# Attention logits in two pieces: key blocks 2 and 3 and then 0 and 1, in place of 1 to 3 and then 0

## The chip, the cores and the metric
The kernel runs on one core of one Trainium2 chip. The metric is the device time of one execution in microseconds; smaller is better. Engines are named as in the profile: PE is TensorE, ACT is ScalarE, DVE is VectorE, POOL is GpSimd, SP issues the DMAs.

## The reference
A decoder trunk of two layers over 512 tokens of width 1024, all in float32. Each layer is a half-step SwiGLU feed-forward, a mixer, and a second half-step feed-forward, each with its modulated RMS norm and gate. The mixer of layer 0 is a causal convolution module. The mixer of layer 1 is stick-breaking attention with 16 heads of width 64, and only this is touched:

```python
z = jnp.einsum('bhqd,bhkd->bhqk', qb, kf)
mask = (key_pos[None, :] < t[:, None])[None, None]
neg_log_keep = jnp.where(mask, jax.nn.softplus(z), 0.0)
rcs = lax.cumsum(neg_log_keep, axis=3, reverse=True)
suffix = jnp.concatenate([rcs[..., 1:], jnp.zeros_like(rcs[..., :1])], axis=-1)
a = jnp.where(mask, jnp.exp(jax.nn.log_sigmoid(z) - suffix), 0.0)
return jnp.einsum('bhqk,bhkd->bhqd', a, vf)
```

So each head needs the logits z, their softplus, a sum of the softplus over all later keys that the query may see, and one exponential.

## The kernel before, in words
Every matrix product is made of products of a high and a low part in the fp32r type. The kernel has one program for each engine, and an engine works through its own in order; semaphores join them. The order around the change is written out by hand.

**Layout.** Keys lie on the 128 partitions and queries along the columns. Key block c (c from 0 to 3) can be seen by the queries of its own block and of the later ones, so it has 512 - 128 c columns: 512, 384, 256 and 128, 1280 in all. One head's logits lie in three PSUM banks of 512 columns from z_base(t); odd and even heads t take different halves (banks 0 to 2 and 3 to 5), banks 6 and 7 take the output of the values. In SBUF a head's 1280 columns lie close together in sp_abs (two buffers, by t modulo 2), sp_hi, sp_lo (one each) and a_f (four, by t modulo 4).

**Pieces.** The columns of a head are worked on in two pieces, PIECE[0] and PIECE[1]. Before the change piece 0 is columns 512 to 1280 (blocks 1, 3 and 2, in banks 1 and 2) and piece 1 columns 0 to 512 (block 0, in bank 0).

**One head, piece by piece.**
1. TensorE, logits(t, p), L1823: mask matmuls write a very negative number on the diagonal blocks (L1843 two blocks at once, L1847 one), and two matmuls for each key block add the logits (L1853); z_done. It first waits until the exponential weights(t-2, p) has read the same banks (a_done).
2. The magnitude of z into sp_abs: of piece 0 by ScalarE's Abs (L904), of piece 1 by VectorE in magnitude(t) (L1450).
3. ScalarE: Exp (L908) and Ln (L910) on it, in place.
4. VectorE: softplus(t, p) (L1457) adds the positive part of z; sp_parts(t, p) splits the result into sp_hi (L1468) and sp_lo (L1470). Those of piece 0 wait until all of suffix(t-1) is done (cum_done).
5. TensorE, suffix(t, p), L1858: subtracts the softplus of the later keys from z, with sp_hi first and sp_lo second; L1864 takes the diagonal parts of two blocks in one matmul, L1867 all others; cum_done.
6. ScalarE, weights(t, p), L887: exp of what stands in PSUM then, into a_f; a_done.
7. TensorE, values(c2), L1873, once for two heads: the product with v (L1883). ScalarE (o_high, L881) and VectorE (o_low, L1474) split its result for the output projection.

**Order.** TensorE: for each t: logits(t+1, 0), suffix(t, 0), logits(t+1, 1), suffix(t, 1), and after an even t from 2 on values(t/2 - 1). ScalarE: for each t: Abs, Exp, Ln of piece 0, weights(t-1, 0), Exp, Ln of piece 1, weights(t-1, 1), and after an odd t from 3 on o_high. VectorE: for each t from 1 on: magnitude(t), softplus(t, 0), sp_parts(t, 0), softplus(t, 1), sp_parts(t, 1), then after an even t up to 10 split_qk (L1406, L1407) and after an odd t from 3 on o_low. For t = 0 magnitude and softplus(0, 1) stand ahead of sp_parts(0, 0). GpSimd computes the low part for split_qk (L647), and SP's DMAs (L541 to L552) bring q and k of the next two heads into stk, for which the next split_qk waits. The output projection (L1520 to L1522 with wsp[0]) follows suffix(15, 1) on TensorE, and SP loads its further weights after the last cum_done.

Of the kernel before, what the change touches and what calls it, by code (L numbers as in the profile page):

```python
# [25 lines left out]
P = 128  # L26
S = 512
# [27 lines left out]
GW = 512  # L55
NFFN = 4

PIECE = [slice(512, 1280), slice(0, 512)]
QL = S + (S - P) + P + (S - 2 * P)


# [38 lines left out]
def trunk(nc, x_in, up_in, down_in, mix_in, ada_in, mod_in, vec_in, dw_in, dwb_in, con_in, ind_in, sel_in, out):  # L100
    ctx = ExitStack()
    with ctx:
# [39 lines left out]
        with ExitStack() as scope:  # L142
            def ov(name, shape, dt=F32):
                return scope.enter_context(nc.sbuf_tensor(name, shape, dt))
# [24 lines left out]
        with ExitStack() as scope:  # L169
# [5 lines left out]
            a_f = ov("a_f", [P, 4, QL])  # L175
            qk = ov("qk", [P, 2 * KD, S])
            v_f = ov("v_f", [P, 4, D])
            con = ov("con", [P, 4, P], F32R)
# [38 lines left out]
        zps = ps[:, :, :].rearrange("p b s -> p (b s)")  # L217
# [121 lines left out]
        def z_base(t):  # L339

            return 3 * S * ((t + 1) % 2)

        def z_of(t, p):

            base = z_base(t)
            return zps[:, base + PIECE[p].start:base + PIECE[p].stop]

        def spread_bank(b):

# [308 lines left out]
        def _(act):  # L658
# [195 lines left out]
            def v_copy(s, c):  # L854
                if c < 3:
                    act.wait_ge(vchunk_done, 3 * (s // 11) + c + 1)
                else:
                    act.wait_ge(slab_done, N_QKV + s + 1)
                act.activation(v_f[:, c, S * (s // 11):S * (s // 11) + S], v_bank(s, c), ACT.Copy).then_inc(vf_done, 1)
# [23 lines left out]
            def weights(t, p):  # L883
                act.wait_ge(cum_done, 2 * t + p + 1)
                if t >= 4 and p == 0:
                    act.wait_ge(av_done, t // 2 - 1)
                act.activation(a_f[:, t % 4, PIECE[p]], z_of(t, p), ACT.Exp).then_inc(a_done, 1)  # L887

            act.add_instruction(mybir.InstLoadActFuncSet(
                name=nc.get_next_instruction_name(), engine=mybir.EngineType.Activation, act_func_set_id=EXP_LN_SET))  # L890
            for t in range(HEADS):
                if t == 0:
                    v_copy(11, 0)
                    v_copy(11, 1)
                    act.wait_ge(bc_done, 2 * KD)
                for p in range(2):
                    if t == 0 and p == 1:
                        v_copy(11, 2)
                    w = sp_abs[:, t % 2, PIECE[p]]
                    if p == 0:  # L900
                        act.wait_ge(z_done, 2 * t + 1)
                        if t >= 2:
                            act.wait_ge(splo_done, 2 * (t - 2) + 1)
                        act.activation(w, z_of(t, 0), ACT.Abs).then_inc(ln_step, 1)  # L904
                        act.wait_ge(ln_step, 5 * t + 1)
                    else:
                        act.wait_ge(abs_done, t + 1)
                    act.activation(w, w, ACT.Exp, scale=-1.0).then_inc(ln_step, 1)  # L908
                    act.wait_ge(ln_step, 5 * t + 2 * p + 2)
                    act.activation(w, w, ACT.Ln, bias=ones[:, 0:1]).then_inc(ln_step, 1)  # L910
                    if t == 0 and p == 1:
                        v_copy(11, 3)
                    if t >= 1:
                        weights(t - 1, p)
                if t % 2 and t >= 3:
                    o_high((t - 3) // 2)
# [12 lines left out]
        def _(dve):  # L929
# [517 lines left out]
            def magnitude(t):  # L1447

                dve.wait_ge(z_done, 2 * t + 2)
                dve.tensor_scalar(sp_abs[:, t % 2, PIECE[1]].bitcast(U32), z_of(t, 1).bitcast(U32), SIGNLESS, None,  # L1450
                                  ALU.bitwise_and).then_inc(abs_done, 1)

            def softplus(t, p):

                w = sp_abs[:, t % 2, PIECE[p]]
                dve.wait_ge(ln_step, 5 * t + 2 * p + 3)
# [3 lines left out]
            def sp_parts(t, p):  # L1460

                w = sp_abs[:, t % 2, PIECE[p]]
                if t == 0 and p == 0:
# [53 lines left out]
        def _(pe):  # L1517
# [296 lines left out]
                    pe.wait_ge(vf_done, 4)  # L1814
                pe.matmul(spread_bank(b), sel[:, b % KD, :], y_both[:, :], start=True, stop=True).then_inc(bc_done, 1)

            at_key = [0, S, 2 * S, 2 * S - P]

            def span(base, c, q0):

                return slice(base + at_key[c] + q0 - P * c, base + at_key[c] + S - P * c)

            def logits(t, p):  # L1823


                base = z_base(t)
                blocks = ((1, 3, 2), (0,))[p]
                c2, half = t // 2, t % 2
                at = stk[c2 % 2]
                pe.wait_ge(stk_s[c2 % 2], 96 * (c2 // 2 + 1))  # L1830
                if half == 1:
                    pe.wait_ge(stkq_s[c2 % 2], 32 * (c2 // 2 + 1))
                if t == 0:
                    pe.wait_ge(conr_done, 2)
                    pe.wait_ge(qkn_done, 2 * KD)
                    pe.wait_ge(vf_done, 4)
                if t == 1:
                    pe.wait_ge(vf_done, 7)
                if t >= 2:
                    pe.wait_ge(a_done, 2 * (t - 2) + p + 1)  # L1840
                if p == 0:
                    diagonals = zps[:, base + S:base + 2 * S].rearrange("p (n q) -> p n q", n=4)[:, 0:4:3, :]
                    pe.matmul(diagonals, con[:, 0, :],  # L1843
                              con[:, 1, :].rearrange("p (n q) -> p n q", n=1).broadcast_to((P, 2, P)),
                              start=True, stop=False, skip_group_check=True)
                first = base + at_key[(2, 0)[p]]
                pe.matmul(zps[:, first:first + P], con[:, 0, :], con[:, 1, :], start=True, stop=False,  # L1847
                          skip_group_check=True)
                for c in blocks:
                    keys = slice(P * c, P * (c + 1))  # L1850
                    seen = slice(P * c, S)
                    for part in range(2):
                        last = pe.matmul(zps[:, span(base, c, P * c)], at[:, half, keys],  # L1853
                                         at[:, 2 + 2 * half + part, seen], start=False, stop=False,
                                         skip_group_check=True)
                last.then_inc(z_done, 1)

            def suffix(t, p):  # L1858

                base = z_base(t)  # L1860
                for part in (sp_hi, sp_lo):
                    pe.wait_ge(sphi_done if part is sp_hi else splo_done, 2 * t + p + 1)
                    if p == 0:
                        pe.matmul(zps[:, base + S:base + 2 * S], con[:, 2, :], part[:, S:2 * S], start=False,  # L1864
                                  stop=(part is sp_lo), skip_group_check=True)
                    for c, later in (((1, 2), (1, 3), (2, 2), (2, 3)), ((0, 0), (0, 1), (0, 2), (0, 3)))[p]:
                        last = pe.matmul(zps[:, span(base, c, P * later)],  # L1867
                                         con[:, 2 if later == c else 3, :],
                                         part[:, span(0, later, P * later)],
                                         start=False, stop=(part is sp_lo), skip_group_check=True)  # L1870
                last.then_inc(cum_done, 1)

            def values(c2):  # L1873

                pe.wait_ge(a_done, 4 * c2 + 4)
                if c2 == 0:
                    pe.wait_ge(vf_done, 8)
                if c2 >= 2:
                    pe.wait_ge(o_done, c2 - 1)
                for c in range(4):  # L1880
                    for half in range(2):
                        cols = slice(P * c2 + HD * half, P * c2 + HD * (half + 1))
                        last = pe.matmul(ps[HD * half:HD * half + HD, 6 + c2 % 2, P * c:S], v_f[:, c, cols],  # L1883
                                         a_f[:, (2 * c2 + half) % 4, span(0, c, P * c)], start=(c == 0), stop=(c == 3),
                                         skip_group_check=True)
                last.then_inc(av_done, 1)

            for s in range(12):
                n = N_QKV + s
# [38 lines left out]
            for t in range(HEADS):  # L1928
                for p in range(2):
                    if t + 1 < HEADS:  # L1930
                        logits(t + 1, p)
                    suffix(t, p)
                if t % 2 == 0 and t >= 2:
                    values(t // 2 - 1)
# [77 lines left out]
```

## Time and profile before

| | us |
|---|---|
| median of 3 runs | 1951.51 |
| lowest, highest | 1951.27, 1951.62 |
| the profiled execution | 1952.25 |
| its span in the profile | 1950.4 |
| granted TensorE clock, mean | 0.999 |

The profile is one execution, and its span leaves out some 1.9 us around the instructions. In the timeline a row is a run of instructions of one line: its start, its time, the engine, the line, and how many; the mean of a group of matmuls is longer than the distance between two of them, since they are pipelined. The attention's head loop runs from about 1447 to 1540 us.

### The profile page before, as it was taken

The page shows a single profiled execution, that of the slowest core. Times are in us where ns is not written, and L with a number is a line of the kernel's source. Part 1 is how long each engine was busy: PE and PEld are TensorE (multiplying, and loading weights), DVE is VectorE, ACT ScalarE, POOL GpSimd, SP SyncE. Part 2 cuts the span into 40 slices and gives each one's busy share as a digit, 9 for nine tenths or more (in the row PEclk, how much of TensorE's full clock was granted, in tenths as well). Part 3 has the DMA queues.
Part 4 walks back from the last instruction along what each step waited for, and adds up shares of the span by engine and source line. Part 5 has one row for each costly group of instructions (what it writes and reads, how often), then busy time and mean ns, then how long its engine had stood idle before and what let it go on. Part 6 is the DMA issues. An engine that isn't in the chain of part 4 may idle for free.

```text
span 1950.4 us, 23638 instructions
## 1 busy us (share of the span) xinstructions
PE 1923.8 (99%) x9211; PEld 1553.7 (80%) x9211; DVE 1075.6 (55%) x1323; ACT 663.4 (34%) x744; POOL 150.9 (8%) x101
## 2 busy tenths in 40 slices
PE   6999999999999999999999999999999999999999
PEld 5888888876578888888888888887777788888887
DVE  4655555589877555533756553255579673333322
ACT  4423222242354222322422222224259653232211
POOL 0100001121411000001100000111022030000000
PEclk9999999999999999999999999999999999999999
DMA  9455554536313555533255552232245323222232
GB/s 393 161 190 197 194 181 143 188 114 179 107 66 119 202 186 199 169 115 99 98 194 185 202 178 90 101 124 97 86 119 130 104 81 108 100 94 99 76 103 87
DMA packets 59992, 275.86 MB, mean 141 GB/s; under 512 B 8480, under 2 KB 9120, under 8 KB 43168
## 3 DMA queue, kind: packets, MB, share of 16 engines
q1 hardware_dynamic: 56864, 270.88, 41.0%
q10 hardware_dynamic: 3072, 4.23, 0.9%
q8 instruction: 36, 0.59, 0.1%
q14 instruction: 20, 0.16, 0.0%
HBM read 251.94 MB, written 2.10 MB: 130 GB/s over the span
## 4 chain that ended last, share of the span: by engine, by line
PE 93%; DMA 2%; DVE 2%; ACT 1%; issue 1%; SPq 1%; ACTq 0%; POOL 0%; DVEq 0%
PE ps L1520 27%; PE ps L1521 27%; PE ps L1522 27%; PE ps L1761 2%; PE ps L1541 2%; DMA raw<-up_d 1%; PE ps L1548 1%; PE ps L1867 1%; PE ps L1883 1%; PE ps L1560 1%; PE ps L1561 1%; PE ps L1566 1%; PE ps L1853 1%; DMA stage<-ada_d 1%; SPq L492 0%
## 5 line engine op out<-in xcount | busy, mean ns | idle before, releaser
L1520 PE MATMUL ps<-h_hi,w 128*128 128x512 f32 x1552 | 606.0, 390 | 1.1 <-DVE h_lo L1033 1.1
L1521 PE MATMUL ps<-h_lo,w 128*128 128x512 f32 x1552 | 604.0, 389 | 0.0
L1522 PE MATMUL ps<-h_hi,w 128*128 128x512 f32 x1552 | 603.9, 389 | 0.0
L1520 PEld LDWEIGHTS ps<-h_hi,w 128*128 128x128 f32 x1552 | 291.3, 188 | 68.9 <-issue 7.9
L1522 PEld LDWEIGHTS ps<-h_hi,w 128*128 128x128 f32 x1552 | 291.3, 188 | 60.8
L1521 PEld LDWEIGHTS ps<-h_lo,w 128*128 128x128 f32 x1552 | 291.3, 188 | 59.9
L933 DVE TENSOR_TENSOR w<-raw,w 128x1408 fp32r<-128x1408 f32 (+1 forms) x104 | 201.0, 1932 | 207.9 <-ACT w L664 207.8
L664 ACT ACTIVATE w<-raw 128x1408 fp32r<-128x1408 f32 (+1 forms) x104 | 164.7, 1584 | 414.9 <-PE ps L1522 403.4
L1520 PE MATMUL ps<-g_hi,w 128*128 128x512 f32 x704 | 273.9, 389 | 0.0
L1521 PE MATMUL ps<-g_lo,w 128*128 128x512 f32 x704 | 273.9, 389 | 0.0
L1522 PE MATMUL ps<-g_hi,w 128*128 128x512 f32 x704 | 273.9, 389 | 0.0
L725 ACT ACTIVATE act_tmp<-ps 128x512 f32<-128x512 f32 x84 | 50.2, 597 | 547.6 <-PE ps L1522 531.5
L940 DVE SCALAR_TENSOR_TENSOR ada_raw<-ada_raw 128x1024 f32<-128x1024 f32 x128 | 163.3, 1276 | 96.1 <-DMA ada_raw<-mod_t_d 96.1
L1133 DVE TENSOR_TENSOR act_tmp<-act_tmp,ps 128x512 f32<-128x512 f32 x84 | 57.8, 688 | 280.2 <-ACT act_tmp L725 280.2
L1141 DVE TENSOR_TENSOR w<-raw,w 128x2048 fp32r<-128x2048 f32 x76 | 174.0, 2290 | 29.8 <-ACT w L730 29.2
L1522 PEld LDWEIGHTS ps<-g_hi,w 128*128 128x128 f32 x704 | 132.1, 188 | 27.5
L1521 PEld LDWEIGHTS ps<-g_lo,w 128*128 128x128 f32 x704 | 132.1, 188 | 27.4
L1520 PEld LDWEIGHTS ps<-g_hi,w 128*128 128x128 f32 x704 | 132.1, 188 | 27.4
L730 ACT ACTIVATE w<-raw 128x2048 fp32r<-128x2048 f32 x76 | 144.6, 1903 | 0.0
L1114 DVE SCALAR_TENSOR_TENSOR x<-ps,gt,x 128x512 f32<-128x512 f32 x48 | 35.8, 749 | 126.5 <-PE ps L1522 126.5
L727 ACT ACTIVATE g_hi<-act_tmp 128x512 f32 (+1 forms) x84 | 53.1, 632 | 70.9 <-DVE act_tmp L1133 70.9
L579 POOL TENSOR_TENSOR ss<-ss,sq_tmp 128x512 f32<-128x512 f32 x30 | 53.8, 1792 | 265.1 <-ACT sq_tmp L671 264.1
(221 smaller groups left out, 1674.7 us busy)
## 6 DMA issues: line engine op xcount, KB each, us to landing
raw<-up_d SPq DMA_DIRECT2D x88, 1024.0 KB, 4.8
ada_raw<-mod_t_d SPq DMA_DIRECT2D x128, 512.0 KB, 4.0
raw<-down_d SPq DMA_DIRECT2D x64, 704.0 KB, 4.1
raw<-mix_d SPq DMA_DIRECT2D x28, 1024.0 KB, 4.8
stage<-ada_d SPq DMA_DIRECT2D x12, 1024.0 KB, 20.2
stk<-parted SPq DMA_DIRECT2D x32, 256.0 KB, 3.9
stk<-parted SPq DMA_DIRECT2D x32, 128.0 KB, 2.3
u_blk<-u SPq DMA_DIRECT2D x48, 64.5 KB, 2.1
```

Of the source, the lines that this page charges most:

```text
L579: pool.tensor_tensor(ss[:, :], a, sq_tmp[:, c % 2, :], ALU.add).then_inc(ss_step, 1)
L664: act.activation(wsp[n % 2][:, 0, 0:cols], raw[n % 2][:, 0:cols], ACT.Copy).then_inc(hi_done, 1)
L725: act.activation(tmp, pair[s][0], ACT.Silu).then_inc(silu_done, 1)
L727: act.activation(g_hi[:, 2 * i + s, :], tmp, ACT.Copy).then_inc(ghi_done, 1)
L730: act.activation(wsp[s][:, 0, :], raw[s][:, :], ACT.Copy).then_inc(hi_done, 1)
L933: dve.tensor_tensor(wsp[n % 2][:, 1, 0:cols], raw[n % 2][:, 0:cols], f32(wsp[n % 2][:, 0, 0:cols]), ALU.subtract) \
L940: dve.scalar_tensor_tensor(out=ada_tile, in0=ada_tile, scalar=1.0, in1=e_row, op0=ALU.mult, op1=ALU.mult, accum_out=dst).then_inc(ada_step, 1)
L1133: dve.tensor_tensor(tmp, tmp, pair[s][1], ALU.mult).then_inc(g_full, 1)
L1141: dve.tensor_tensor(wsp[s][:, 1, :], raw[s][:, :], f32(wsp[s][:, 0, :]), ALU.subtract) \
L1520: pe.matmul(dst, a_hi_, b_hi_, start=start, stop=False, skip_group_check=True)
L1521: pe.matmul(dst, a_hi_, b_lo_, start=False, stop=False, skip_group_check=True)
L1522: return pe.matmul(dst, a_lo_, b_hi_, start=False, stop=stop, skip_group_check=True)
```

## The change
The head's columns are divided otherwise. Piece 0 is now key blocks 2 and 3, 384 columns, and piece 1 blocks 1 and 0, 896 columns. In PSUM block 3 moves from behind block 1 (bank 1) to behind block 2 (bank 2), so that piece 0 is all in bank 2 (columns 1024 to 1408 of the three banks) and piece 1 in banks 0 and 1; Z_PIECE has these columns. In SBUF the columns stay close together (kept_at): block 0, block 1, block 3, block 2. The matmul over two diagonals (L1843 and L1864 of before) now takes blocks 2 and 3; blocks 1 and 0 have one mask matmul each. The order of the steps on every engine stays.

```diff
-PIECE = [slice(512, 1280), slice(0, 512)]
+PIECE = [slice(896, 1280), slice(0, 896)]
+Z_PIECE = [slice(1024, 1408), slice(0, 896)]
...
-            return zps[:, base + PIECE[p].start:base + PIECE[p].stop]
+            return zps[:, base + Z_PIECE[p].start:base + Z_PIECE[p].stop]
...
-            at_key = [0, S, 2 * S, 2 * S - P]
+            at_key = [0, S, 2 * S, 2 * S + 2 * P]
+            kept_at = [0, S, 2 * S - P, 2 * S + P]
...
+            def kept(c, q0):
+
+                return slice(kept_at[c] + q0 - P * c, kept_at[c] + S - P * c)
...
-                blocks = ((1, 3, 2), (0,))[p]
+                blocks = ((3, 2), (1, 0))[p]
...
-                    diagonals = zps[:, base + S:base + 2 * S].rearrange("p (n q) -> p n q", n=4)[:, 0:4:3, :]
+                    diagonals = zps[:, base + 2 * S:base + 2 * S + 3 * P].rearrange("p (n q) -> p n q", n=3)[:, 0:3:2, :]
...
-                first = base + at_key[(2, 0)[p]]
-                pe.matmul(zps[:, first:first + P], con[:, 0, :], con[:, 1, :], start=True, stop=False,
-                          skip_group_check=True)
+                else:
+                    for c in blocks:
+                        first = base + at_key[c]
+                        pe.matmul(zps[:, first:first + P], con[:, 0, :], con[:, 1, :], start=True, stop=False,
+                                  skip_group_check=True)
...
-                        pe.matmul(zps[:, base + S:base + 2 * S], con[:, 2, :], part[:, S:2 * S], start=False,
+                        pe.matmul(zps[:, base + 2 * S:base + 2 * S + 3 * P], con[:, 2, :], part[:, PIECE[0]], start=False,
                                   stop=(part is sp_lo), skip_group_check=True)
-                    for c, later in (((1, 2), (1, 3), (2, 2), (2, 3)), ((0, 0), (0, 1), (0, 2), (0, 3)))[p]:
+                    for c, later in (((2, 3),), ((1, 1), (1, 2), (1, 3), (0, 0), (0, 1), (0, 2), (0, 3)))[p]:
                         last = pe.matmul(zps[:, span(base, c, P * later)],
                                          con[:, 2 if later == c else 3, :],
-                                         part[:, span(0, later, P * later)],
+                                         part[:, kept(later, P * later)],
...
-                                         a_f[:, (2 * c2 + half) % 4, span(0, c, P * c)], start=(c == 0), stop=(c == 3),
+                                         a_f[:, (2 * c2 + half) % 4, kept(c, P * c)], start=(c == 0), stop=(c == 3),
```

## Rows read from the trace of the kernel before

**Rows 1.** The page: busy time by engine; the chain that ended last.
```profile
PE 1923.8 (99%) x9211; PEld 1553.7 (80%) x9211; DVE 1075.6 (55%) x1323; ACT 663.4 (34%) x744; POOL 150.9 (8%) x101
...
PE 93%; DMA 2%; DVE 2%; ACT 1%; issue 1%; SPq 1%; ACTq 0%; POOL 0%; DVEq 0%
```

**Rows 2.** Stretches: length, busy PE, PEld, DVE, ACT, POOL, clock, DMA.
```profile
1457.00:1460.60 3.60, 3.60 (x14) 3.21 (x14) 2.52 (x4) 2.53 (x5) 0.00 (x0) 0.53 0.96 228
...
1479.00:1490.70 11.70, 11.36 (x76) 9.29 (x75) 11.43 (x18) 10.64 (x15) 2.64 (x2) 1.00 0.59 137
...
1525.80:1537.50 11.70, 11.36 (x77) 9.36 (x75) 10.29 (x16) 10.53 (x15) 0.00 (x0) 1.00 0.01 1
```

**Rows 3.** Groups by form, 1467.3 to 1537.5 us: count, busy us, mean ns, idle.
```profile
L1470 DVE TENSOR_TENSOR sp_lo<-sp_abs,sp_hi 128x768 fp32r<-128x768 f32 x13 | 12.5, 958 | 0.5
L1457 DVE SCALAR_TENSOR_TENSOR sp_abs<-ps,sp_abs 128x768 f32<-128x768 f32 x12 | 11.4, 951 | 0.1
L910 ACT ACTIVATE sp_abs<-sp_abs,ones 128x768 f32<-128x768 f32 x12 | 11.3, 940 | 0.4
...
L908 ACT ACTIVATE sp_abs<-sp_abs 128x768 f32<-128x768 f32 x12 | 10.2, 847 | 0.4
L904 ACT ACTIVATE sp_abs<-ps 128x768 f32<-128x768 f32 x12 | 9.7, 807 | 3.7 <-PE ps L1853 3.7
...
L887 ACT ACTIVATE a_f<-ps 128x768 f32<-128x768 f32 x12 | 9.5, 790 | 0.0
L1457 DVE SCALAR_TENSOR_TENSOR sp_abs<-ps,sp_abs 128x512 f32<-128x512 f32 x13 | 8.9, 684 | 0.0
L910 ACT ACTIVATE sp_abs<-sp_abs,ones 128x512 f32<-128x512 f32 x12 | 8.7, 723 | 0.4
L1470 DVE TENSOR_TENSOR sp_lo<-sp_abs,sp_hi 128x512 fp32r<-128x512 f32 x12 | 8.3, 693 | 0.4
L1450 DVE TENSOR_SCALAR sp_abs<-ps 128x512 uint32<-128x512 uint32 x12 | 8.2, 684 | 1.0 <-PE ps L1853 1.0
...
L908 ACT ACTIVATE sp_abs<-sp_abs 128x512 f32<-128x512 f32 x12 | 7.5, 623 | 0.2
L887 ACT ACTIVATE a_f<-ps 128x512 f32<-128x512 f32 x12 | 6.9, 578 | 0.0
...
L1468 DVE CAST sp_hi<-sp_abs 128x512 fp32r<-128x512 f32 x12 | 5.1, 427 | 0.4
```

**Rows 4.** Timeline of DVE, heads 11 and 12: start, us, line.
```profile
1510.70 0.42 DVE L1406 CAST parted<-qk 128x512 fp32r<-128x512 f32 x1
...
1511.37 0.69 DVE L1450 TENSOR_SCALAR sp_abs<-ps 128x512 uint32<-128x512 uint32 x1
...
1512.96 1.30 DVE L1468 CAST sp_hi<-sp_abs 128x768 fp32r<-128x768 f32 x1
...
1516.95 0.68 DVE L1474 TENSOR_TENSOR h_lo<-ps,h_hi 128x512 fp32r<-128x512 f32 x1
...
1519.13 0.56 DVE L1468 CAST sp_hi<-sp_abs 128x768 fp32r<-128x768 f32 x1
```

**Rows 5.** Timeline of PE, logits(12) and suffix(11); the wait is bracketed.
```profile
1514.06 0.38 PE L1843 MATMUL ps<-con 128*128 128x256 f32 x1
...
1515.19 0.39 PE L1864 MATMUL ps<-sp_hi,con 128*128 128x512 f32 x1
...
1517.15 0.75 PE L1867 MATMUL ps<-sp_hi,con 128*128 128x512 f32 x4
...
1518.90 0.36 PE L1843 MATMUL ps<-con 128*128 128x256 f32 x1 [0.34 <-ACT a_f L887]
```

**Rows 6.** Timeline of DVE, where the loop starts.
```profile
1451.67 0.43 DVE L1406 CAST parted<-qk 128x512 fp32r<-128x512 f32 x1 [1.37 <-DMA stk<-parted]
...
1452.34 0.69 DVE L1450 TENSOR_SCALAR sp_abs<-ps 128x512 uint32<-128x512 uint32 x1
```

**Rows 7.** Timeline of PE: the wait before suffix(1,0); the projection's start.
```profile
1455.27 0.50 PE L1864 MATMUL ps<-sp_hi,con 128*128 128x512 f32 x1 [2.09 <-DVE sp_hi L1468]
...
1540.11 0.45 PE L1520 MATMUL ps<-h_hi,w 128*128 128x512 f32 x1
```

## The prediction
> **What bounds the kernel now.** I read the engines' totals and the chain that ended last first: TensorE is busy for 99% of the span and holds 93% of the chain, so over the whole kernel a microsecond counts only where TensorE is made to wait [rows 1]. Then the table of stretches, cut at the period of the attention loop, because the change touches nothing else. Two heads (a pair: values() runs once in two heads) take 11.70 us; TensorE is busy for 11.36 of them, VectorE for 11.43 while split_qk still runs, ScalarE for 10.64 [rows 2]. Three engines are nearly full at once, so totals don't decide here, the dependences do. In the timeline TensorE waits once in a pair for ScalarE's first-piece exponential (0.34 us, L1843 behind L887) [rows 5].
>
> The order of VectorE's instructions is fixed: magnitude(t), softplus(t,0), sp_hi and sp_lo of piece 0, softplus(t,1), sp_hi and sp_lo of piece 1, then split_qk or o_low, then magnitude(t+1). So there is a second loop, through the second piece alone: magnitude(t), ScalarE's Exp and Ln of piece 1, softplus(t,1), sp_hi, sp_lo, magnitude(t+1). It needs nothing from TensorE as long as the logits are early. With 512 columns it is a duration plus some 0.034 us for each dependent step: 0.684 + 0.034, 0.623 + 0.033, 0.723 + 0.032, 0.684 + 0.034, 0.427 + 0.034, and 0.693 - 0.083 for the last, behind which an independent instruction starts early: 3.92 us [rows 3]. With split_qk (0.67, 1510.70 to 1511.37) or o_low (0.60; L1474 starts 0.60 ahead of its successor) it is under 4.6 us a head [rows 4], against the 5.85 that a head takes. It is covered by 1.3 us a head now.
>
> **The change, part by part.** The instructions stay the same in number on every engine: for each head three mask matmuls, eight of the logits (six and two by piece before, four and four after), and nine suffix matmuls for each of sp_hi and sp_lo (five and four before, two and seven after). What moves is block 1 (384 columns) from piece 0 to piece 1.
>
> TensorE. Before, the logits of piece 0 stream 1920 columns with their masks in 1.13 us (1514.06 to 1515.19), and the suffix of piece 0 and the logits of piece 1 together 2560 + 1152 columns in 1.96 us (to 1517.15) [rows 5]: 0.53 to 0.59 ns a column, weight loads included. After: logits 1024 columns (0.68 us, small matmuls, so I take the high end and a little more) and 2048 (1.1 us); suffix 1024 (0.53) and 4096 (2.05). The sum is 4.35 us a head, where it was 4.34. Zero for TensorE's own work, down to -0.1 or up to +0.2 us a head if the many short matmuls overlap better or worse.
>
> ScalarE. Abs of piece 0 drops from 768 to 384 columns: 0.807 less 1.5 times the 0.214 that 256 columns cost in L887, some 0.49; it gives 0.32 us a head back. Exp, Ln and the final Exp only trade columns between pieces, so their sum stays. ScalarE has 1.1 us in a pair to spare already [rows 2], so this buys nothing unless ScalarE is the bound.
>
> VectorE. magnitude grows from 512 to 896 columns. softplus costs 951 ns for 768 and 684 for 512, so 1.04 ns a column, and magnitude becomes 0.684 + 0.40 = 1.08 us [rows 3]. The other VectorE work is the same in sum. That is +0.40 us a head of plain work, +6.4 us over 16 heads if the queue alone counted.
>
> The loop through piece 1. No instruction of 896 or 384 columns is in the trace; two sizes of nearly every link are. By the line through 512 and 768 [rows 3], at 896 columns: magnitude 1.08, Exp 0.96, Ln 1.05, softplus 1.08, sp_hi 0.63 (0.427 at 512, 0.56 at 768 where nothing holds it up [rows 4]), sp_lo 1.09. With the same 0.034 a step and 0.083 off the last: 1.118 + 0.997 + 1.080 + 1.116 + 0.661 + 1.006 = 5.98 us. With split_qk 6.65, with o_low 6.58, together 13.2 us a pair against 11.70. The bounds: if each link kept its price at 768 (magnitude the 0.684 of its only row), the loop would be 5.0 plus 0.6, under 5.85, and cost nothing; if each grew in proportion from 512, 6.8 plus 0.6, and the change would cost 21 us. The line lies near the 768 rows, 128 columns beyond them, and all kinds of instruction here are a constant plus a slope, so I take the line.
>
> Do the other links fit under that? Lay magnitude(8) at 0. VectorE: softplus(8,0) 1.00, sp_hi 1.58, sp_lo 1.98, done 2.5. ScalarE: Exp(8,1) 1.12, Ln 2.11, done 3.16, then softplus(8,1) 3.20, so VectorE idles for 0.7 us in front of it. sp_hi(8,1) 4.31, sp_lo 4.97, split_qk 5.98, magnitude(9) 6.65. TensorE: suffix(8,0) waits for sp_hi at 1.98 and for sp_lo at 2.55; logits(9,1) waits for the 0.90 us final Exp of (7,1), which stands behind Ln(8,1) on ScalarE, until 4.0, ends 5.1, is readable at 5.3: 1.3 us before magnitude(9) wants it. suffix(8,1) ends 7.15, 0.9 us before sp_hi(9,0) needs its release. TensorE then idles 2.2 us of 13.2. The GpSimd lock, behind which sp_hi(t,0) takes 1.30 in place of 0.56 us [rows 4], held it until 2.9 us after magnitude's start; in the new order it would let sp_hi(9,0) go at about the same point, and sp_lo(9,0) ends just as Ln(9,1) does, 3.2 us after magnitude(9): no term of its own. Without split_qk (t of 12 and 14) a head takes 5.98. SP's restacking DMAs wait for logits and qklo as before, and a longer head gives them more room.
>
> **The sum.** The first loop is set by the landing of stk, for which VectorE waits until 1451.67; with the change sp_lo(0,1) ends about then (worked forward with the same prices: 1451.7), so magnitude(1) stays at 1452.34 [rows 6]. To magnitude(15): 14 x 5.98 = 83.7, five split_qk 3.35, six o_low 3.6: 1543.0. From there softplus(15,1) at +3.20, sp_hi +4.31, sp_lo done at +6.1, and the second half of suffix(15,1), 1.05 us, ends at +7.15: 1550.1. Before, suffix ended and the output projection began at 1540.11 [rows 7]. +10.0 us. Behind it everything (the loads that wait for cum_done, the projection, the last feed-forward) is released by that point and moves as a whole.
>
> **The clock.** After TensorE had waited 2.09 us for L1468 [rows 7], the granted clock fell to its lower level (1.2 GHz): it reads 0.53 over the 3.6 us from 1457.00 [rows 2]. Such a stretch does 1.9 us of work in 3.6, 1.7 us lost on TensorE, of which the 0.9 of slack worked out above takes the half; 0.8 us a time would come through. The kernel now has one of them and, after it, waits of 0.34 us at clock 1.00. The changed loop idles TensorE for 2.2 us in a pair, in three parts. I add 0.5 us for one more such stretch or so: 1952.25 + 10.5 = 1962.75 for an execution like the profiled one. That one lay 0.74 above the median of the runs, so I predict a median of 1962.0. The Trainium skill ("TensorE: Matmul & The Clock Gate", "A second HAM failure mode: psum-queue depth-cycling") reports a kernel in which frequent short idles between groups of matmuls made the clock swing between the two levels. By that rule the lower clock would come back in every pair; the trace's short waits at 1.00 speak against it, its one fall after 2.09 us for it.
>
> **The rivals.** First, that clock swing: one stretch at the lower level in each of 8 pairs, 0.5 to 0.8 us each past the slack, on top of 10.0: +14 to +16, 1966. For it: 2.2 us idle close together; against it: TensorE is full for the other 11 us.
> Second, only VectorE's extra work counts and the loop overlaps better than I lay it out (Exp and Ln shorter at 896, or VectorE already so full that its own sum is the bound): +6.4, 1957.9. For it: VectorE's 11.43 of 11.70; against it: its 0.7 us of waiting for Ln.
> Third, the cover holds: the links at 896 cost little more than at 768, the loop stays below 5.85 a head, and TensorE sets the period: no change, 1951.5.
> Fourth, faster: the wait in L1843 is gone, since a 384-column Abs, Exp, Ln and final Exp release logits(t+2,0) 1.3 us earlier. Where that wait and the small one for sp_lo set the pair, 0.34 + 0.1 us x 8 comes off: 1948. It decides only if the loop through piece 1 takes less than 5.7 us a head with its extras, that is, if its links were 0.9 us a head below the line.
>
> **How the numbers follow.** My forecast, with none to three falls of the clock, +9.5 to +12.5: 0.66. The swing 0.14. The queue sum 0.12. The cover 0.05, of which 0.01 goes to slightly slower. Faster 0.03. A difference under 0.2% (3.9 us) can't be told from none here. Slower 0.93, same 0.04, faster 0.03. The range runs from the queue sum, 1957.5, to the beginning of the swing, 1966.
>
> **What would show it.** A pair takes 13.2 us while split_qk runs, 12.6 after; magnitude at 1.08, softplus at 1.08, sp_lo at 1.09 us; VectorE idle some 0.7 us ahead of softplus(t,1), ended by Ln; the wait at L1843 gone, and new waits of TensorE for sp_hi(t,0) and for the final Exp of piece 1, some 2 us in a pair; the output projection begins 10 to 12 us later and the rest takes as long as before. I am wrong if VectorE has no idle time there, if the period is below 12.5, or if the granted clock in the loop lies well below 1.

## The result and the profile after

| | before | after |
|---|---|---|
| median, us | 1951.39 (4 runs) | 1963.59 (4 runs) |
| lowest to highest | 1950.51 to 1951.62 | 1962.73 to 1964.67 |
| profiled execution | 1952.25 | 1963.35 |
| its span | 1950.4 | 1961.5 |

The ratio is 1.0062, with a 95% interval of 1.005 to 1.0075: slower by 12.2 us, where 10.5 was forecast. Timed again on another chip, the changed kernel had a median of 1962.81 (four runs, 1962.49 to 1965.23); over all eight runs it is 1963.2, 11.8 us above before. One execution each of three of the experiments below took 2142, 3598 and 4959 us; the ratios leave them out, and no median moves by more than 0.03 us by them.

The page of the kernel after, totals and chain, beside [rows 1]: TensorE's share of the chain falls from 93% to 91%, and VectorE's rises from 2% to 5%.

```profile
PE 1931.8 (98%) x9211; PEld 1558.4 (79%) x9211; DVE 1081.0 (55%) x1323; ACT 657.9 (34%) x744; POOL 151.6 (8%) x101
...
PE 91%; DVE 5%; ACT 2%; DMA 1%; issue 1%; POOL 0%; SPq 0%; DVEq 0%; ACTq 0%
```

The stretches of after, columns as in [rows 2]: two heads from magnitude(5) to magnitude(7), and two from magnitude(12), where split_qk is over.

```profile
1478.28:1491.51 13.23, 11.70 (x69) 9.38 (x68) 12.31 (x18) 9.88 (x15) 2.64 (x3) 0.91 0.51 120
...
1525.50:1538.05 12.55, 11.96 (x78) 9.78 (x77) 10.99 (x15) 10.42 (x17) 0.00 (x0) 1.00 0.09 23
```

A pair takes 13.23 us where it took 11.70, and 12.55 once split_qk is over. The clock column reads 0.91 in the first row, so TensorE did some of its work there at the lower level. The changed kernel was run again (below); this is the same pair in that profile, at the upper level throughout:

```profile
1477.87:1491.09 13.22, 11.69 (x77) 9.41 (x75) 12.30 (x19) 9.89 (x15) 2.63 (x3) 1.00 0.51 120
```

Groups by form of after, 1467.3 to 1550 us, columns as in [rows 3]:

```profile
L1471 DVE TENSOR_TENSOR sp_lo<-sp_abs,sp_hi 128x896 fp32r<-128x896 f32 x13 | 14.2, 1093 | 0.5
L1458 DVE SCALAR_TENSOR_TENSOR sp_abs<-ps,sp_abs 128x896 f32<-128x896 f32 x13 | 14.2, 1089 | 4.0 <-ACT sp_abs L911 3.7
L911 ACT ACTIVATE sp_abs<-sp_abs,ones 128x896 f32<-128x896 f32 x13 | 13.6, 1043 | 0.4
L1451 DVE TENSOR_SCALAR sp_abs<-ps 128x896 uint32<-128x896 uint32 x12 | 13.0, 1085 | 0.6 <-PE ps L1861 0.6
...
L909 ACT ACTIVATE sp_abs<-sp_abs 128x896 f32<-128x896 f32 x12 | 11.4, 952 | 16.1 <-DVE sp_abs L1451 16.1
...
L1469 DVE CAST sp_hi<-sp_abs 128x896 fp32r<-128x896 f32 x13 | 8.2, 627 | 0.4
```

Each size was forecast within 0.01 us. The idle column has the loop: ScalarE waits 16.1 us for the magnitude ahead of Exp (it had waited 0.2 us there [rows 3]), and VectorE 3.7 us for Ln ahead of softplus.

VectorE's timeline of after in the even head 6, and TensorE's from the head before it on. The bracket has the idle time before the instruction and what ended it.

```profile
1484.87 1.08 DVE L1451 TENSOR_SCALAR sp_abs<-ps 128x896 uint32<-128x896 uint32 x1
...
1486.84 0.56 DVE L1471 TENSOR_TENSOR sp_lo<-sp_abs,sp_hi 128x384 fp32r<-128x384 f32 x1
1488.04 1.09 DVE L1458 SCALAR_TENSOR_TENSOR sp_abs<-ps,sp_abs 128x896 f32<-128x896 f32 x1 [0.64 <-ACT sp_abs L911]
...
1491.51 1.08 DVE L1451 TENSOR_SCALAR sp_abs<-ps 128x896 uint32<-128x896 uint32 x1
```

```profile
1481.50 0.62 PE L1861 MATMUL ps<-stk 128*128 128x128 f32 x4
...
1482.48 0.39 PE L1855 MATMUL ps<-con 128*128 128x128 f32 x2
...
1485.81 0.62 PE L1861 MATMUL ps<-stk 128*128 128x128 f32 x4
1486.86 0.44 PE L1872 MATMUL ps<-sp_hi,con 128*128 128x384 f32 x1 [0.43 <-DVE sp_hi L1469]
...
1488.96 0.60 PE L1855 MATMUL ps<-con 128*128 128x128 f32 x2 [1.00 <-ACT a_f L888]
```

Magnitude to magnitude is 6.64 us here, with VectorE idle for 0.64 in the middle and softplus 3.17 us after magnitude. TensorE's wait at L1843 [rows 5] is gone, and it waits for sp_hi and for the final exponential of piece 1 in its place. The brackets leave out a part of these waits, because the last matmul before one is counted as busy on into it. The starts show all of it: from L1861 of piece 0 to L1855 of piece 1, the same matmuls in both heads, it is 0.98 us in odd head 5 (no wait bracketed) and 3.15 in head 6, so TensorE waits 2.17 us in a pair.

The projection begins at 1551.23, 11.1 us after 1540.11 [rows 7], and from there to the end of the span both kernels take 410.3 us:

```profile
1551.23 0.45 PE L1521 MATMUL ps<-h_hi,w 128*128 128x512 f32 x1
```

### The profile page after: what moved, and what is told of

Its sections match the earlier page's. It is cut to its first block, busy times and chain, and to the rows that moved or that the text cites. A ratio compares the mean times of both kernels' runs of the same rounds, so it can differ in the third digit from the quotient of the medians.

```text
span 1961.5 us, 23638 instructions
## 1 busy us (share of the span) xinstructions
PE 1931.8 (98%) x9211; PEld 1558.4 (79%) x9211; DVE 1081.0 (55%) x1323; ACT 657.9 (34%) x744; POOL 151.6 (8%) x101
## 4 chain that ended last, share of the span: by engine, by line
PE 91%; DVE 5%; ACT 2%; DMA 1%; issue 1%; POOL 0%; SPq 0%; DVEq 0%; ACTq 0%
PE ps L1521 27%; PE ps L1522 27%; PE ps L1523 27%; PE ps L1762 2%; PE ps L1542 2%; PE ps L1562 1%; PE ps L1567 1%; PE ps L1561 1%; PE ps L1549 1%; DVE sp_abs L1458 1%; DVE sp_abs L1451 1%; DVE sp_hi L1469 1%; DMA stage<-ada_d 1%; DVE sp_lo L1471 1%; ACT sp_abs L909 0%
```

## The experiments

Twelve runs follow, the first of them the changed kernel once more. "The loop" is magnitude(t), Exp, Ln, softplus, sp_hi, sp_lo of piece 1, magnitude(t+1); a loop period is the time from one magnitude to the next. "The gap" is the stretch in an even head in which VectorE waits for Ln. A fall is a stretch in which TensorE's granted clock is at its lower level.

### The changed kernel again


> The changed kernel as it is, for runs on the same chip as the experiments beside it. 1963.6 us again (four runs lay between 1962.7 and 1964.7). If the falls of TensorE's granted clock differ from run to run, the mean clock of the runs (0.995 to 0.998 so far) goes down where the time goes up: some 0.4 us for each fall by the profile. The profile again has magnitude(t) to magnitude(t+1) at 6.65 us after an even head with split_qk, 6.58 after an odd head, and VectorE idle by 0.64 us ahead of softplus(t,1) in even heads.

1962.81 us. In this profile the loop periods are 6.64 and 6.58 again. The clock fell twice, at other places (1449.6 and 1528.1 us): the period at the first is 6.41 for 5.98, and the two at the second are 6.39 and 7.31 for 5.98 and 6.58. The timed runs reach from 1962.5 to 1965.2 though their mean clock reads 0.997 in all four, so the mean clock of a run is too coarse to price a fall.

### One instruction more on VectorE: in the gap, and in the loop
```diff
                 sp_parts(t, 0)
+                if t and t % 2 == 0:      # first kernel: in the gap
+                    dve.tensor_tensor(junk[:, 0, :], x[:, 0, :], x[:, 1, :], ALU.add)
                 if t:
                     softplus(t, 1)
                 sp_parts(t, 1)
+                if t and t % 2 == 0:      # second kernel: in the loop
+                    dve.tensor_tensor(junk[:, 0, :], x[:, 0, :], x[:, 1, :], ALU.add)
```


> The changed kernel with one more VectorE instruction in each of the 7 even heads from 2 on: a sum of 512 columns (0.69 us, 0.61 to the next start) into a tile that nobody reads, put between sp_lo(t,0) and softplus(t,1), where VectorE idles for 0.64 us. Theory (the loop magnitude, Exp, Ln, softplus, sp_hi, sp_lo of piece 1 sets the pace): the instruction fills the gap and costs nothing, 1963.6, at most 1 us more; the period of a pair stays 13.23. Rival (VectorE's work in sum is the bound): 7 x 0.61 = +4.3, 1967.9.

> The same extra VectorE instruction in the same 7 even heads, put behind sp_lo(t,1) and so ahead of the next magnitude, inside the loop. Theory: all of it shows, 7 x 0.61 = +4.3 us, 1967.9, though the last of them (t of 14) counts only once as well. Rival (VectorE's work in sum): +4.3 too. The two theories differ in the pair of this run and the one with the instruction in the gap: 4.3 us apart by the loop, equal by the sum.

In the gap: 1964.43 us (1964.16 to 1964.83), +1.6 over the changed kernel on the same chip. In the loop: 1966.71 (1966.18 to 1967.51), +3.9. VectorE in an even head, first with the instruction in the gap, then in the loop:

```profile
1486.83 0.68 DVE L1488 TENSOR_TENSOR junk<-x 128x512 f32<-128x512 f32 x1
1487.56 1.09 DVE L1459 SCALAR_TENSOR_TENSOR sp_abs<-ps,sp_abs 128x896 f32<-128x896 f32 x1
```

```profile
1489.32 1.09 DVE L1459 SCALAR_TENSOR_TENSOR sp_abs<-ps,sp_abs 128x896 f32<-128x896 f32 x1 [0.64 <-ACT sp_abs L912]
...
1492.12 0.69 DVE L1491 TENSOR_TENSOR junk<-x 128x512 f32<-128x512 f32 x1
1492.72 0.42 DVE L1408 CAST parted<-qk 128x512 fp32r<-128x512 f32 x1
```

In the gap the wait for Ln is gone and the even head stays at 6.65 us; in the loop the wait stays and the head is 7.25. By the profiles the same work at two places costs 0 and 0.6 us a head: VectorE's sum is not the bound. The times alone say it less clearly: the two medians are 2.3 us apart where 4.3 was expected, because the first kernel is 1.6 us up all the same, more than the theory's 1. Its profile has a place for that. The clock falls twice, as in the changed kernel. At 1449.6 us the period is 6.20 for 5.98. Behind the second fall VectorE waits 2.00 us for suffix(8,1); that loop period is 8.45 us and the next 7.07, for 6.58 and 6.64. Stretch and wait:

```profile
1501.40:1504.80 3.40, 3.11 (x10) 2.95 (x11) 3.33 (x6) 2.04 (x5) 0.73 (x1) 0.50 0.00 0
```

```profile
1507.79 0.36 DVE L1470 CAST sp_hi<-sp_abs 128x384 fp32r<-128x384 f32 x1 [2.00 <-PE ps L1878]
```

Whether each of its runs has such a fall isn't shown, so the cause of the 1.6 us stays open.

### One instruction more on ScalarE: in the loop, and in its gap
```diff
                     else:
+                        if t:      # second kernel: in the gap
+                            act.activation(junk[:, 1, :], x[:, 1, :], ACT.Copy)
                         act.wait_ge(abs_done, t + 1)
                     act.activation(w, w, ACT.Exp, scale=-1.0).then_inc(ln_step, 1)
+                    if t and p == 1:      # first kernel: in the loop
+                        act.activation(junk[:, 1, :], x[:, 1, :], ACT.Copy)
```


> The changed kernel with one more ScalarE instruction in each head from 1 on: a copy of 512 columns from x to a tile that nobody reads, between Exp and Ln of piece 1. It should take some 0.6 us and put the next start back by some 0.5. ScalarE idles 3 us of 13.2 in a pair, so by the sum of work it costs nothing. Theory (loop): ScalarE's step is in the loop, 15 x 0.47 = +7 us, 1970.6. Rival (VectorE's work in sum is the bound): no change, 1963.6.

> The same ScalarE copy of 512 columns in each head from 1 on, put ahead of the wait for magnitude(t), where ScalarE idles for 1.3 to 1.85 us. Theory (loop through piece 1): 0, 1963.6. If ScalarE's work in sum or its releases of piece 0 counted, +7 as in the other place. The two places of the one instruction should differ by about 7 us.

In the loop 1968.3 us (+5.5 over the changed kernel on its chip), in the gap 1963.33 (within its noise). ScalarE, in the loop and in the gap:

```profile
1487.84 0.95 ACT L910 ACTIVATE sp_abs<-sp_abs 128x896 f32<-128x896 f32 x1 [1.29 <-DVE sp_abs L1454]
1488.69 0.61 ACT L912 ACTIVATE junk<-x 128x512 f32<-128x512 f32 x1
1489.21 1.03 ACT L914 ACTIVATE sp_abs<-sp_abs,ones 128x896 f32<-128x896 f32 x1
```

```profile
1484.41 0.62 ACT L910 ACTIVATE junk<-x 128x512 f32<-128x512 f32 x1
1485.81 0.95 ACT L912 ACTIVATE sp_abs<-sp_abs 128x896 f32<-128x896 f32 x1 [0.78 <-DVE sp_abs L1454]
```

From Exp to Ln is 1.37 us where it was 0.99 in the changed kernel: 0.38 a head, for a 0.61 us copy (the copy starts before Exp has ended, and Ln before the copy has). 15 x 0.38 = 5.7, the measured 5.5; the 0.47 of the expectation was too much. In the changed kernel ScalarE idles for a quarter of the pair (9.89 busy us of 13.22), and work added to it inside the loop still lengthens every head. This speaks against a bound by VectorE's sum again, since VectorE got no work.

### o_low moved into the gap
```diff
                 sp_parts(t, 0)
+                if t >= 4 and t % 2 == 0:
+                    o_low((t - 4) // 2)
                 if t:
                     softplus(t, 1)
...
-                if t % 2 and t >= 3:
+                if t == HEADS - 1:
                     o_low((t - 3) // 2)
```


> The changed kernel with o_low(c) (0.60 us of VectorE) taken from behind sp_lo(t,1) of odd heads and put between sp_lo(t+1,0) and softplus(t+1,1) of the even head after it, where VectorE idles for 0.64 us. The same instructions, one place moved. Theory (loop): the loop loses 0.6 us in six odd heads, -3.6 us, 1960.0; a pair goes from 13.23 to 12.6. Rival (VectorE's work in sum): no change, 1963.6.

1959.47 us (1958.88 to 1960.12): -3.7 against the 1963.2 of the changed kernel's eight runs. Nothing was left out, one instruction stands elsewhere. Up to head 11 the odd heads take 5.98 us from magnitude to magnitude, the six bare links (6.58 with o_low), and the even ones 6.64 as before: five times 0.6, 3.0 us. The sixth move gives nothing. Heads 13 and 14 take 6.15 and 6.39, together the 12.54 that they took before it (6.57 and 5.98), and VectorE now waits 0.58 us for suffix(13,1). The median fell by 0.7 us more than the profile's 3.0; fewer falls (one in its profile, two in the changed kernel's) could be the cause, which isn't shown. VectorE in head 6, where softplus follows o_low with no wait, and in head 14:

```profile
1485.73 0.68 DVE L1475 TENSOR_TENSOR h_lo<-ps,h_hi 128x512 fp32r<-128x512 f32 x1
1486.39 1.09 DVE L1458 SCALAR_TENSOR_TENSOR sp_abs<-ps,sp_abs 128x896 f32<-128x896 f32 x1
...
1535.37 0.36 DVE L1469 CAST sp_hi<-sp_abs 128x384 fp32r<-128x384 f32 x1 [0.58 <-PE ps L1877]
```

### The places in PSUM alone
```diff
+            return zps[:, base + S:base + 3 * S].rearrange("p (n q) -> p n q", n=2)[:, :, 0:3 * P]
...
-            at_key = [0, S, 2 * S, 2 * S - P]
+            at_key = [0, S, 2 * S, 2 * S + 2 * P]
+            kept_at = [0, S, 2 * S - P, 2 * S + P]
...
-                    for c, later in (((1, 2), (1, 3), (2, 2), (2, 3)), ...
+                    for c, later in (((2, 3), (1, 1), (1, 2), (1, 3)), ...
```


> The kernel before with the change's places in PSUM alone: block 3 behind block 2 (bank 2) in place of behind block 1 (bank 1), the two-diagonal matmul over blocks 2 and 3, but the old division (blocks 1 to 3, 768 columns, then block 0, 512). Piece 0 is read as two runs of 384 columns. The same number of instructions and columns. Theory (the division makes the whole difference): 1951.5, within 1 us. Rival (the banks matter: piece 0 of before shared bank 1 between blocks 1 and 3): some of the 12 us shows here, or the kernel is faster by up to 2 us.

1951.38 us, beside 1951.43 of before; the ratio is 0.9999 (0.999 to 1.0008). The places in PSUM make no difference beyond that interval, some 2 us either way, so the 12 us, or at least 10 of them, are in the division. Its profile had no fall of the clock in the head loop, which is used below.

### TensorE's waits filled
```diff
+            def fill(t, n):
+                ...
+                for _ in range(n):
+                    pe.matmul(ps[:, 6 + c2 % 2, :], con[:, 0, :], con[:, :, :].rearrange("p n q -> p (n q)"),
+                              start=True, stop=True, skip_group_check=True)
...
+                    if p == 0 and t % 2 == 0 and t >= 2:
+                        fill(t, 3)
                     suffix(t, p)
```
(and `fill(t, 4)` ahead of logits(t+1, 1))

> The changed kernel with seven more matmuls of 512 columns in each even head from 2 on, into the bank that the next values() overwrites: three (0.69 us) where TensorE waits for sp_hi(t,0), four (0.92) where it waits for the exponential of piece 1. The profile of the changed kernel has two stretches of 3.4 us at the lower clock in the head loop, each followed by a loop period 0.43 to 0.45 us too long. Theory: TensorE keeps its clock through the head loop, and 0.9 us comes back, 1962.7, with runs less spread than the 1962.7 to 1964.7 of the changed kernel; the fillers delay suffix(t,0) by up to 0.3 us, which is not on the loop. Rival (the 1 to 2 us above the worked out 10 have nothing to do with the clock, or the fillers stand in TensorE's way): 1963.6 or up to 3 us more.

1962.61 us (1961.62 to 1962.85); the ratio to before is 1.0056 (1.0043 to 1.007). The same stretch, first of the changed kernel, then of this one:

```profile
1464.50:1538.00 73.50, 67.79 (x415) 54.89 (x414) 65.88 (x93) 55.07 (x83) 13.19 (x10) 0.95 0.47 108
```

```profile
1464.50:1538.00 73.50, 72.99 (x456) 58.47 (x456) 68.12 (x95) 54.73 (x83) 13.16 (x10) 1.00 0.47 108
```

The clock stays at its upper level, and every loop period in it is the undisturbed 6.64, 6.58 or 5.98. There is a fall at 1449.6 us, before the first filler (6.43 for 5.98). The gain of 0.6 us against the eight runs is less than their spread, so the time doesn't prove it. Nor does the profile show that the fillers kept the clock up: with o_low moved and no filler at all, and TensorE as little busy as in the changed kernel, it stayed up over the same stretch too:

```profile
1464.50:1538.00 73.50, 67.82 (x436) 54.92 (x435) 70.27 (x98) 58.30 (x88) 13.11 (x10) 1.00 0.47 108
```

What is shown is that the waits could be filled without lengthening the loop; what this does for the clock stays open.

### The magnitude shared, on top of o_low moved
```diff
                     else:
+                        if t:
+                            act.wait_ge(z_done, 2 * t + 2)
+                            ...
+                            act.activation(sp_abs[:, t % 2, S:2 * S - P], zps[:, z_base(t) + S:z_base(t) + 2 * S - P],
+                                           ACT.Abs).then_inc(absb_done, 1)
```
(VectorE's magnitude takes the other 512 columns)

> The changed kernel with two cuts into the loop: o_low in the gap of the even heads, as in the run before (which gave 1959.5), and the magnitude of piece 1 shared: VectorE takes the 512 columns of block 0, ScalarE the 384 of block 1 with an Abs (0.49 us) that it does while it waits. By the loop alone the links fall by 0.40 us a head from there, 14 x 0.4 = 5.6: 1954; a pair would take 11.8. But at that pace the other links are near: ScalarE gets 0.5 us more a head, and sp_hi(t,0) waits for suffix(t-1,1) with under 1 us to spare, so a part may stay behind: 1954 to 1957. If the loop were not the cause, ScalarE's new work and an unchanged VectorE sum less 0.4 a head would leave 1957 at best only by VectorE's sum, and the period would not fall in the heads where VectorE idles.

1957.67 us, 1.8 below the run with o_low alone, where the loop by itself gave 5.6; just outside the 1954 to 1957. From magnitude(3) to magnitude(5), two heads take 12.58 us, and in the run before this one 12.63: while split_qk runs, the shorter link gives nearly nothing. The waits of the head loop (us in total, times, longest) and VectorE's timeline of head 7 say why:

```profile
DVE sp_hi L1478 <- PE ps L1886: 4.3, 8, 1.0
```

```profile
1490.98 1.52 DVE L1480 TENSOR_TENSOR sp_lo<-sp_abs,sp_hi 128x384 fp32r<-128x384 f32 x1
```

VectorE waits for suffix(t-1,1) before sp_hi of piece 0 eight times. In the changed kernel it did so five times for 3.0 us, four of them behind its two falls; here the clock stays up in this stretch. The prediction had 0.9 us of slack there, at a loop longer by 0.4 us a head. And behind split_qk sp_lo of 384 columns takes 1.52 us for 0.56 (GpSimd is busy from 1489.23 to 1492.07), so softplus follows it with no wait for Ln in brackets. The next bounds lie close behind the loop.

### VectorE's extra work without the rest
```diff
                 if t:
                     magnitude(t)
+                    dve.tensor_tensor(junk[:, 0, 0:320], x[:, 0, 0:320], x[:, 1, 0:320], ALU.add)
```


> The kernel before with the VectorE work that the change adds and nothing else of it: a sum of 320 columns behind each magnitude from head 1 on, some 0.41 us to the next start, as much as magnitude grows by 384 columns. It prices the rival of the prediction (VectorE's sum, +6.4). The loop through piece 1 would be 3.9 + 0.4 + 0.6 = 4.9 us a head, still covered. VectorE is full in the pairs with split_qk (11.43 of 11.70), so I expect +0.8 us in each of five pairs and little in the last two: +4, 1955.5. If the sum is all that counted in the change: +12. If VectorE is covered: 0.

1955.59 us, +4.3; ratio 1.0021 (1.0011 to 1.0031). In the kernel before, the 0.4 us a head that the change adds to VectorE cost 4.3 us. A period of two heads with split_qk goes from 11.70 to 12.34. So about a third of the loss would be there without any loop; the loop takes its place and is the larger, they don't add.

### Two tries at a faster kernel
Both start from the kernel before. The first fills the wait ahead of suffix(1,0):
```diff
+                    if t == 1 and p == 0:
+                        for _ in range(8):
+                            pe.matmul(ps[:, 6, :], con[:, 0, :], con[:, :, :].rearrange("p n q -> p (n q)"),
+                                      start=True, stop=True, skip_group_check=True)
                     suffix(t, p)
```


> The kernel before with eight matmuls of 512 columns (1.9 us) put into TensorE's wait of 2.1 us before suffix(1,0), into the bank that values(0) overwrites. In the profile of before the granted clock fell after this wait and the next two loop periods were 6.01 and 6.23 us; in the run with the layout alone it did not fall and they were 5.57 and 5.51, and the projection began 1.3 us earlier. Theory: the clock stays up and the kernel gains 0 to 1.3 us (some runs of before may have no fall either): 1950.6. Rival: the fillers end later than sp_hi(1,0) and delay it: no change or up to 0.5 us more.

1950.6 us; the ratio of 0.9996 has an interval of 0.9987 to 1.0005, so it isn't shown to be faster. The wait of 2.09 us [rows 7] is 0.27, the clock doesn't fall, and the loop periods there are 5.61 and 5.51 in place of 6.01 and 6.24. But the layout alone had the wait and no filler, and its clock stayed up too (periods of 5.57 and 5.51), so one profile doesn't show that the filler kept it up. The filled wait, and then the layout's:

```profile
1452.21 2.00 PE L1934 MATMUL ps<-con 128*128 128x512 f32 x8
1454.48 0.50 PE L1864 MATMUL ps<-sp_hi,con 128*128 128x512 f32 x1 [0.27 <-DVE sp_hi L1468]
```

```profile
1455.11 0.44 PE L1875 MATMUL ps<-sp_hi,con 128*128 128x384 f32 x1 [2.12 <-DVE sp_hi L1474]
```

The second also gives values() out by the head:
```diff
-                if t % 2 == 0 and t >= 2:
-                    values(t // 2 - 1)
+                if 1 <= t < HEADS - 1:
+                    values((t - 1) // 2, ((t - 1) % 2,))
...
```
(values() takes the halves as an argument, issues their matmuls only, and waits for the exponential of its own head)

> The kernel before with the same fillers, and values() given out by the head: half of its matmuls (1.15 us) after suffix(t,1) of each head from 1 on in place of all of them (2.3 us) after even heads. TensorE now waits 0.34 us for the exponential of piece 0 in the heads without values() and not in the others; spread evenly it should not wait there. But VectorE is nearly full in the pairs with split_qk. Worked out from the order of the queues: -0.6 us against the fillers alone, 1950.0; at best 8 x 0.4 = 3 us less if TensorE's waits were all that holds a pair.

1963.13 us, +11.8, where -0.6 against the fillers alone was expected: a plain miss. values() for one head takes as long as for two. TensorE before (16 matmuls, two heads), then in this run (8 matmuls, one head):

```profile
1500.06 2.37 PE L1883 MATMUL ps<-a_f,v_f 128*64 128x512 f32 x16
1502.36 0.38 PE L1843 MATMUL ps<-con 128*128 128x256 f32 x1
```

```profile
1485.80 2.37 PE L1883 MATMUL ps<-a_f,v_f 128*64 128x512 f32 x8
1488.09 0.39 PE L1843 MATMUL ps<-con 128*128 128x256 f32 x1
```

The next matmul starts 2.30 and 2.29 us after values(). By these two times the work that I halved was work that had run two abreast. TensorE is busy for 13.5 us in a pair of 13.5, where it was 11.36 of 11.70, and each head takes 6.7 us.

No version beats the kernel before by more than can be told.

## Why the prediction was right, step by step

**The loop through piece 1 sets the pace: right and shown.** By the profiles, instructions inside it cost their step and outside it nothing (0.6 and 0 us a head on VectorE, 0.38 and 0 on ScalarE), and moving o_low out of it takes 3.7 us off the median. The forecast of 5.98 us bare, 6.65 with split_qk and 6.58 with o_low came out as 5.98, 6.64 and 6.58.

**The line through two sizes: right.** All six links at 896 columns lie within 0.01 us of it. Both bounds (the price at 768, growth in proportion) were far off.

**The other links: right in kind.** VectorE idles 0.64 us (0.7 forecast) for Ln; TensorE waits for sp_hi(t,0) and the final exponential, 2.17 us in a pair (2.2 forecast). Its own work then is 11.05 us in a pair (13.22 - 2.17), and whether it grew a little can't be read from the time, which the loop sets. The 0.9 us of slack ahead of sp_hi(9,0) is of the right size as well: a fall of 3.40 us at 0.50 takes 1.7 us from TensorE, and behind the first one VectorE waits 0.90 us for suffix (at 1493.96).

**Start and end of the loop: right to 0.1 us.** magnitude(1) at 1452.43 (1452.34 forecast), and from magnitude(15) to the projection 7.20 (7.15). Everything behind it moved as a whole.

**The clock: falls came as forecast, their price and cause less sure.** The forecast was 10.0 without and 10.5 with the clock; the profiled pair of spans is 11.1 apart, the medians 12.2 or, with all runs, 11.8. Of the 1.1 us beyond 10.0, the two falls account for 0.95 (the periods of heads 7 and 11 are 7.07 and 7.04, both for 6.58) and the start and end for 0.14. The stretches:

```profile
1489.00:1492.40 3.40, 3.40 (x11) 3.11 (x12) 3.33 (x6) 1.71 (x4) 1.06 (x1) 0.50 0.00 0
1516.20:1519.60 3.40, 3.40 (x14) 3.11 (x13) 3.37 (x6) 1.52 (x4) 1.31 (x1) 0.52 0.09 19
```

My price of 0.8 us for a fall was the slack worked out once. In the loop periods of the profiles it is 0.22 to 2.3: 0.46 and 0.49 here, 0.43 and 1.14 in the second run of this kernel, 0.22 and 2.3 in the run with the instruction in VectorE's gap. What sets it isn't shown. I also counted the fall in the profile of before as part of it without asking what it cost there. The run with the layout alone had none, and its projection began at 1538.80, 1.3 us earlier than before's. Without falls on either side the projection thus begins 11.5 us later (1551.23 - 0.95 - 1538.80). The forecast had the end of the changed loop right (1550.1, and 1550.28 without its falls), but took it from an end of before that had a fall in it; against a loop without one the 10.0 is too small by the 1.3. Both profiles of the changed kernel have two falls and those of the four kernels with one instruction more two or three; before has one, the layout alone none. That falls make the medians differ by more than the two spans fits this, but no run shows it.

**The rivals.** The swing of the clock in every pair did not come: each profile of the changed kernel has two falls in the head loop's eight pairs, and of its eight executions one, at 1965.23, lies 14 us above before. The section of the Trainium skill that I had cited, "TensorE: Matmul & The Clock Gate", "A second HAM failure mode: psum-queue depth-cycling", tells of a swing that keeps coming back, and that isn't seen here. What the two profiles of this kernel show is that the lower clock followed waits with brackets of some 0.43 and 1.00 us in one head three times (falls at 1489.0, 1516.2 and 1528.1), and that the same waits in five other even heads were followed by none. The wait of 2.09 us that the prediction gives as the cause of the fall in before is as doubtful: the layout alone waited 2.12 us there, and its clock stayed up. That short waits bring the falls is likely, since each of these came behind one, but what decides when is open. VectorE's sum is real at +4.3 us but smaller than the loop. The cover did not hold: a head takes 6.6 us with its extras, 0.8 more than the 5.85 under which it would have had to stay. The faster rival's premise came true (the wait in L1843 is gone) and gave nothing, because that wait was no longer in the binding loop.

## What to carry to other kernels

Where several engines are nearly full, don't add up engines; write down each closed loop of dependences through the fixed orders and sum its steps, the ones that cover it now included. Moving work to a piece that goes round such a loop is paid at each of its links (six here), even when it is free in every engine's sum; what isn't part of the loop belongs in its gaps. A one-instruction probe inside and outside the supposed loop tests it in two runs, if the periods in the profile are read beside the times: here the times alone gave 2.3 us of the 4.3 expected.

## What the hardware showed that I had not expected

Matmuls of values() with 64 output columns, issued alternately for the two halves of the partitions of the output, run two abreast, by the time they take: 16 in 2.30 us. Eight for one half alone take 2.29. Halving such a group saved nothing here.

A fall of TensorE's clock followed waits of well under 2 us in a head (brackets of 0.43 and 1.00), but the same waits were followed by none five times, and its price was not fixed: 0.46 and 0.49 us in the changed kernel, 2.3 us in the run with the instruction in VectorE's gap (8.45 and 7.07 for 6.58 and 6.64).
